# A ring of eight raw weight halves and three rounded ones in a mixture-of-experts layer

## The reference

```python
def hier_moe(h, w_coarse, b_coarse, w_fine, b_fine, w_gate, w_up, w_down):
    t = h.reshape(b * n, d)
    ...
    gates = jnp.sum(jax.nn.one_hot(eidx, N_EXPERTS, dtype=jnp.float32) * pe[..., None], axis=1)
    a = (jax.nn.silu(jnp.einsum('td,edf->tef', t, w_gate))
         * jnp.einsum('td,edf->tef', t, w_up) * gates[:, :, None])
    y = jnp.einsum('tef,efd->td', a, w_down)
```

## Time and profile before

| | us |
|---|---|
| median of 3 runs | 905.15 |
| lowest, highest | 894.86, 905.91 |
| the profiled execution, its own time | 903.03 |
| its span | 900.8 |
| TensorE busy in the span | 863.3 (96%) |
| VectorE busy | 680.5 (76%) |
| ScalarE busy | 461.2 (51%) |
| DMA share in the expert loop | 0.95 to 1.00 |

### The profile page before, as it was taken

The page is one execution under the profiler, slowest core; times in us unless marked ns, Lnnn a source line. Parts: engine busy times, 40 slices in busy tenths (PEclk is TensorE's granted clock), DMA queues, the critical chain, the costliest instruction groups (busy, mean ns, idle before and its releaser), DMA issues.

```text
span 900.8 us, 12158 instructions
## 1 busy us (share of the span) xinstructions
PE 863.3 (96%) x4477; PEld 685.4 (76%) x4477; DVE 680.5 (76%) x1018; ACT 461.2 (51%) x693; POOL 229.7 (25%) x210
## 2 busy tenths in 40 slices
PE   4999999999998999999999999999999999999996
PEld 3789999999996555578888667777777767777653
DVE  5557876968856777466888758988888888888678
ACT  6541211111125777534453618786777677776533
POOL 1000000000024777623021231323322332222141
PEclk9899999999999999999999979999999999999999
DMA  9731526424200112152121589999999999998296
GB/s 369 311 120 44 216 67 241 169 89 164 68 29 29 49 48 102 9 210 94 47 94 48 238 290 334 381 381 380 371 379 366 374 371 361 360 366 333 104 377 255
DMA packets 42003, 194.55 MB, mean 216 GB/s; under 512 B 12150, under 2 KB 13110, under 8 KB 25046
## 3 DMA queue, kind: packets, MB, share of 16 engines
q1 hardware_dynamic: 32232, 174.24, 51.5%
q0 software_dynamic: 9712, 19.52, 5.8%
HBM read 182.00 MB, written 26.41 MB: 231 GB/s over the span
## 4 chain that ended last, share of the span: by engine, by line
PE 75%; DMA 7%; DVE 7%; ACT 4%; issue 3%; POOL 2%; POOLq 0%; SPq 0%; DVEq 0%; ACTq 0%
PE PS L968 9%; PE PS L970 8%; PE PS L972 8%; DMA w_gu<-in_w_gu 5%; PE PS L2474 5%; PE PS L2475 5%; PE PS L2476 5%; PE PS L2508 4%; PE PS L1774 3%; PE PS L1776 3%; PE PS L1775 3%; PE PS L1112 3%; PE PS L1081 3%; PE PS L1132 3%; PE PS L2463 2%
## 5 line engine op out<-in xcount | busy, mean ns | idle before, releaser
L2279 DVE TENSOR_TENSOR gu_lo<-w_gu,gu_hi 128x2048 fp32r<-128x2048 f32 x62 | 141.8, 2287 | 28.4 <-ACT gu_hi L2165 28.4
L968 PE MATMUL PS<-h_hi,w_hi 128*128 128x384 f32 (+1 forms) x432 | 148.3, 343 | 2.5 <-DVE h_lo L677 1.9
L2165 ACT ACTIVATE gu_hi<-w_gu 128x2048 fp32r<-128x2048 f32 x62 | 118.9, 1917 | 58.0 <-DMA w_gu<-in_w_gu 57.9
L970 PE MATMUL PS<-h_lo,w_hi 128*128 128x384 f32 (+1 forms) x432 | 147.0, 340 | 0.0
L972 PE MATMUL PS<-h_hi,w_lo 128*128 128x384 f32 (+1 forms) x432 | 146.5, 339 | 0.0
L2474 PE MATMUL PS<-gu_hi,xT_hi 128*128 128x512 f32 x256 | 103.3, 403 | 1.2 <-DVE xT_lo L2338 1.2
L2475 PE MATMUL PS<-gu_lo,xT_hi 128*128 128x512 f32 x256 | 100.4, 392 | 0.0
L2476 PE MATMUL PS<-gu_hi,xT_lo 128*128 128x512 f32 x256 | 100.2, 391 | 0.0
L2109 POOL DMA_INDIRECT y_rows<-yrows,tab x31 | 37.3, 1202 | 211.4 <-DVE yrows L2311 211.4
L968 PEld LDWEIGHTS PS<-h_hi,w_hi 128*128 128x128 f32 x432 | 81.8, 189 | 8.8 <-issue 7.6
L970 PEld LDWEIGHTS PS<-h_lo,w_hi 128*128 128x128 f32 x432 | 82.3, 191 | 0.0
(11 more groups left out here) (290 smaller groups left out, 1746.7 us busy)
## 6 DMA issues: line engine op xcount, KB each, us to landing
w_gu<-in_w_gu SPq DMA_DIRECT2D x64, 1024.0 KB, 13.8
w_d<-in_w_down SPq DMA_DIRECT2D x32, 1024.0 KB, 13.3
wm<-in_w_mod SPq DMA_DIRECT2D x16, 1024.0 KB, 5.3
w_raw<-in_w_in SPq DMA_DIRECT2D x18, 512.0 KB, 6.3
yt<-y_rows SPq DMA_DIRECT2D x9, 1024.0 KB, 15.2
xt<-in_x_all SPq DMA_DIRECT2D x9, 512.0 KB, 3.6
y_all<-yt SPq DMA_DIRECT2D x9, 512.0 KB, 3.0
wm<-in_w_mod SPq DMA_DIRECT2D x2, 2048.0 KB, 12.5
```

What stands on the lines that cost most here:

```text
L968: pe.matmul(o, w_hi[b][:, k, :], h_hi[:, k, tok], start=k == 0, stop=False)
L970: pe.matmul(o, w_hi[b][:, k, :], h_lo[:, k, tok], start=False, stop=False)
L2165: act.activation(gu_hi[n % 2][:, h, :], w_gu[:, n % 3, h, :], ACT.Copy).then_inc(s_hi, 1)
L2279: dve.tensor_tensor(gu_lo[:, n % 3, h, :], w_gu[:, n % 3, h, :], raw(gu_hi[n % 2][:, h, :]), ALU.subtract).then_inc(s_lo, 1)
```

## The change

The raw halves become a ring of eight (six in the places of `w_gu`, two new ones, `gu_raw6` and `gu_raw7`; the low parts likewise), and the rounded halves a ring of three. `gu_hi1` has one half instead of two, `g2row` one row instead of two, and `fg` and the second row of g2 are loaded after the loop into `xrows`. ScalarE rounds the first half of expert n+2 after silu(n), and the second half after the blend; VectorE makes the low part of the first half after product(n). Two counts of the filler matmuls change, and the order of the tiles in the tail.

```diff
                 pe.wait_ge(s_comb, NT + 1)
-                keep_busy(4, 3)
+                keep_busy(6, 3)
                 pe.wait_ge(s_both, 4)
...
-                keep_busy(4, 3)
+                keep_busy(3, 3)
...
-        ORDER = [4, 5, 0, 1, 8, 6, 2, 3, 7]
+        ORDER = [0, 1, 2, 3, 8, 4, 5, 6, 7]
+        RING, HIGHS = 8, 3
+        s_half = [*(s for pair in s_wgu for s in pair), s_xt[0], s_xt[1]]
+        half_base = [0] * 6 + [16 * (NT - NT // 2), 16 * (NT // 2)]
...
+            def high_half(i):
+                return gu_hi1[:] if i % HIGHS == 2 else gu_hi0[:, i % HIGHS, :]
...
+                    sp.wait_ge(s_gx[0], 16)
+                    for i in range(6, RING):
+                        load_half(i)
                     sp.wait_ge(s_gx[1], 16)
-                    sp.dma_start(g2row[:].rearrange("p c n -> p (c n)"),
-                                 mod_g2.to_broadcast([P, 2 * D])).then_inc(s_g2row, 16)
-                    sp.dma_start(fg[:], a["final_g"].to_broadcast([P, D])).then_inc(s_p7, 16)
+                    sp.dma_start(g2row[:], mod_g2[:, 0:D].to_broadcast([P, D])
+                                 ).then_inc(s_g2row, 16)
                     for n in range(NE):
-                        if n + 3 < NE:
-                            for h in range(2):
-                                sp.wait_ge(s_gu, 2 * n + h + 1)
-                                load_gu(n + 3, h)
+                        for i in (2 * n, 2 * n + 1):
+                            if i + RING < 2 * NE:
+                                sp.wait_ge(s_gu, i + 1)
+                                load_half(i + RING)
...
+                    sp.wait_ge(s_turnx, NE)
+                    sp.dma_start(fg, a["final_g"].to_broadcast([P, D])).then_inc(s_p7, 16)
+                    sp.dma_start(g2_ctx, mod_g2[:, D:2 * D].to_broadcast([P, D])
+                                 ).then_inc(s_p7, 16)
...
                     def high(n, h):
-                        act.wait_ge(s_wgu[n % 3][h], 16 * (n // 3 + 1))
-                        if n >= 2:
-                            act.wait_ge(s_gu, 2 * (n - 2) + h + 1)
...
+                        i = 2 * n + h
+                        loaded_half(act, i)
+                        if i >= HIGHS:
+                            act.wait_ge(s_gu, i - HIGHS + 1)
+                        act.activation(high_half(i), raw_half(i), ACT.Copy).then_inc(s_hi, 1)
...
-                        if n + 2 < NE:
-                            high(n + 2, 0)
                         if n == HELD:
                             blend(n - 1)
                         if n:
                             silu(n)
                         if n + 2 < NE:
+                            high(n + 2, 0)
                             xhigh(n + 2)
-                            high(n + 2, 1)
                         if 1 <= n < HELD:
                             blend(n - 1)
+                        if n + 2 < NE:
+                            high(n + 2, 1)
...
                             turned_low(n - 1)
-                        if n + 2 < NE:
-                            low(n + 2, 0)
                         if n == HELD:
                             out(n - 1)
                         if n:
                             product(n)
+                        if n + 2 < NE:
+                            low(n + 2, 0)
                         if n + 2 < NE:
                             xlow(n + 2)
```

More of the change, by code:

```diff
@@ L1968, in build @@
         HELD = NE - 1
-        ORDER = [4, 5, 0, 1, 8, 6, 2, 3, 7]
+        ORDER = [0, 1, 2, 3, 8, 4, 5, 6, 7]
+        RING, HIGHS = 8, 3
+        GU_LAP = len(range(0, 2 * NE, RING))
+        s_half = [*(s for pair in s_wgu for s in pair), s_xt[0], s_xt[1]]
+        half_base = [0] * 6 + [16 * (NT - NT // 2), 16 * (NT // 2)]
         DVE_SUM = ORDER[1]
@@ L1977, in build @@
             sb6 = allocator(st, "right")
-            g2row = sb6("g2row", [P, 2, D])
-            fg = sb6("fg", [P, D])
+            g2row = sb6("g2row", [P, D])
+            with ExitStack() as same:
+                gu_raw6 = allocator(same, "right")("gu_raw6", [P, HALF])
+            gu_lo6 = sb6("gu_lo6", [P, HALF], F32R)
+            fg, g2_ctx = xrows[:, 1, :], xrows[:, 2, :]
             with ExitStack() as same:
@@ L1983, in build @@
             sb6("gu_hi0_again", [P, 2, HALF], F32R)
-            gu_hi = [gu_hi0, sb6("gu_hi1", [P, 2, HALF], F32R)]
+            gu_hi1 = sb6("gu_hi1", [P, HALF], F32R)
+            with ExitStack() as same:
+                gu_raw7 = allocator(same, "right")("gu_raw7", [P, HALF])
+            gu_lo7 = sb6("gu_lo7", [P, HALF], F32R)
             xT_hi = sb6("xT_hi", [P, 2, KD, P], F32R)
@@ L1997, in build, with raw_half, low_half, loaded_half @@
             held_id = sb6("held_id", [P, 1])
-            held_hi, held_lo = gu_hi[1][:, 0, 0:D], gu_hi[1][:, 1, 0:D]
+            held_hi, held_lo = gu_hi1[:, 0:D], gu_hi1[:, D:2 * D]
+            def raw_half(i):
+                s = i % RING
+                return w_gu[:, s // 2, s % 2, :] if s < 6 else [gu_raw6, gu_raw7][s - 6][:]
+            def low_half(i):
+                s = i % RING
+                return gu_lo[:, s // 2, s % 2, :] if s < 6 else [gu_lo6, gu_lo7][s - 6][:]
+            def high_half(i):
+                return gu_hi1[:] if i % HIGHS == 2 else gu_hi0[:, i % HIGHS, :]
+            def loaded_half(eng, i):
+                eng.wait_ge(s_half[i % RING], half_base[i % RING] + 16 * (i // RING + 1))
             def held_rows(t):
@@ L2033, in _, with load_half @@
                     sp.wait_ge(s_tab, 4)
-                    def load_gu(n, h):
-                        sp.dma_start(w_gu[:, n % 3, h, :], a["w_gu"][n, h]
-                                     ).then_inc(s_wgu[n % 3][h], 16)
+                    def load_half(i):
+                        sp.dma_start(raw_half(i), a["w_gu"][i // 2, i % 2]
+                                     ).then_inc(s_half[i % RING], 16)
                     def load_d(n):
                         sp.dma_start(w_d[:, n % 3, :], a["w_down"][n]).then_inc(s_wd[n % 3], 16)
+                    sp.wait_ge(s_gx[0], 16)
+                    for i in range(6, RING):
+                        load_half(i)
                     sp.wait_ge(s_gx[1], 16)
-                    sp.dma_start(g2row[:].rearrange("p c n -> p (c n)"),
-                                 mod_g2.to_broadcast([P, 2 * D])).then_inc(s_g2row, 16)
-                    sp.dma_start(fg[:], a["final_g"].to_broadcast([P, D])).then_inc(s_p7, 16)
+                    sp.dma_start(g2row[:], mod_g2[:, 0:D].to_broadcast([P, D])
+                                 ).then_inc(s_g2row, 16)
                     for n in range(NE):
-                        if n + 3 < NE:
-                            for h in range(2):
-                                sp.wait_ge(s_gu, 2 * n + h + 1)
-                                load_gu(n + 3, h)
+                        for i in (2 * n, 2 * n + 1):
+                            if i + RING < 2 * NE:
+                                sp.wait_ge(s_gu, i + 1)
+                                load_half(i + RING)
                         if 1 <= n and n + 2 < NE:
@@ L2073, in _ @@
                         if t < 6:
-                            sp.wait_ge(s_gu, 2 * (NE - [2, 1, 3][t // 2] + 1))
+                            sp.wait_ge(s_gu, max(i for i in range(2 * NE) if i % RING == t) + 1)
                         else:
@@ L2201, in blend @@
                             act.wait_ge(s_zero, 16)
-                        act.activation(yrows[:, n % 2, :], g2row[:, 0, :], ACT.Identity,
+                        act.activation(yrows[:, n % 2, :], g2row[:], ACT.Identity,
                                        bias=of_ctx[:, n:n + 1], scale=no_ctx[:, n:n + 1]
@@ L2240, in one_expert @@
                         def one_expert(e, m):
-                            act.wait_ge(s_wgu[0][0], 16 * LAP + 16 * m + 16)
-                            act.activation(gu_hi[0][:], w_gu[:, 0, :, :], ACT.Copy
+                            act.wait_ge(s_wgu[0][0], 16 * GU_LAP + 16 * m + 16)
+                            act.activation(gu_hi0[:], w_gu[:, 0, :, :], ACT.Copy
                                            ).then_inc(s_hi, 1)
@@ L2278, in low @@
                         dve.wait_ge(s_hi, 2 * n + h + 1)
-                        dve.tensor_tensor(gu_lo[:, n % 3, h, :], w_gu[:, n % 3, h, :],
-                                          raw(gu_hi[n % 2][:, h, :]), ALU.subtract
+                        i = 2 * n + h
+                        dve.tensor_tensor(low_half(i), raw_half(i), raw(high_half(i)), ALU.subtract
                                           ).then_inc(s_lo, 1)
@@ L2395, in one_expert @@
                             dve.tensor_tensor(gu_lo[:, 0, :, :], w_gu[:, 0, :, :],
-                                              raw(gu_hi[0][:]), ALU.subtract
+                                              raw(gu_hi0[:]), ALU.subtract
```

(12 more changed lines are left out.)

2 lines of the change are left out of this document (removed).

## The result

The changed kernel takes 934.58 us (median of 4, 933.86 to 935.62); beside it the kernel before took 903.05 (median of 4). The ratio on record is 1.038, with a 95% interval of 1.033 to 1.043: 3.8% slower (the two medians divided give 1.035). I had forecast 931 and 2.9% slower. The time lies in my range, the ratio on record lies above it: 937 over the 905.15 that I started from is 1.035.

A forecast was written before the change was run, and what follows sets the result against it. The prediction took TensorE to bound the expert loop, with late weights costing about 5 us. From 903.03 us, + 37.1 (rounded halves) - 5.0 (ring) - 4.5 (fillers) = 930.6, kept as 931; range 908 to 937.

The forecast's parts named there:

- The direction and the mechanism: Expert loop: slower, as three rounded halves make a rounding wait and delay turned_low, stalling TensorE; + 37.1 us.
- G: Mark in the expert loop: the end on TensorE of the first half of gate and up of an expert.
- The opposite rival (the chain hides): Expert loop: the operations queued behind the wait cost TensorE nothing and the larger ring pays; 893.5 us, chance 0.14.
- The period: Time per expert in the loop: claimed to grow from 9.75 to 11.03 us, by 1.28 us.
- The rest of the walk: Loop, from ScalarE's start at G + 0.20 through down_high, down_low, low and turned_low to TensorE going on at G + 6.78.
- "- 4.5" for the fillers: Routing: two more calls of dummy matmuls close TensorE's idle gap and keep its clock up; 4.5 us saved, 0.9 without.
- The start value: Time of the kernel before that the forecast was divided by: 905.15 us, the median of three.
- The prologue, at nothing: Before the loop: two extra halves loaded ahead of the row of g2; priced at 0, up to 3 us if uncovered.
- The ring, - 5: Expert loop: eight raw halves instead of six end the waits for late weights; 5 us saved, bounds 0 and 5.6.
- The loop and the end: Expert loop and tail: + 37.1 us for the rounded halves, - 5.0 for the ring of raw halves, the end at nothing.

The follow-up runs named there:

- e1: Changed kernel with the second half's rounding moved behind turned(n) on ScalarE: 896.06 us, ratio 0.995 to the kernel before.
- e2: Changed kernel with turned_low(n) moved ahead of low(n+2, 1) on VectorE, ScalarE left as it is: 897.07 us, ratio 0.998 to the kernel before.
- e6: Kernel before with the new orders of ScalarE and VectorE, each rounding waiting for one finished half more, buffers unchanged: 937.19 us, ratio 1.042.
- e9: Kernel before with only the new counts of filler matmuls (6 and 3): 900.10 us against 900.03 before, ratio 0.998.
- e4: Changed kernel with the old counts of filler matmuls (4 and 4): 936.07 us, ratio 1.041 to the kernel before.
- e7: Changed kernel with turned_low first on VectorE, as in e2, and six raw halves instead of eight: 894.42 us, ratio 0.996 to the kernel before.
- e11: Same as e10 but with six raw halves instead of eight: 892.94 us, ratio 0.992 to the kernel before.
- e10: Changed kernel with both moves (those of e1 and e2) and the row of g2 loaded first, eight raw halves: 891.90 us, ratio 0.991 to the kernel before.
- e8: Same kernel as e10, measured in an earlier group: 891.34 us, ratio 0.991 to the kernel before.
- e5: Kernel before with only the new orders of ScalarE and VectorE, buffers and waits unchanged: 897.2 us, ratio 0.996.

## Why the prediction was right and where it was off

**The direction and the mechanism were right.** That three places make high(n+2, 1) wait for G, and that down_high, down_low, low and turned_low stand behind it, is shown by e1, e2 and, from the other side, by e6. The opposite rival (the chain hides) is what e1 and e2 measure, at 896 and 897 against its 893.5; what had to be changed for it was the place of one operation.

**The period was a little short.** I had 11.03 us; it is 11.09. ScalarE starts 0.26 after G, not 0.20, which I had taken from SP's queue. The rest of the walk from there to TensorE's restart (6.58 us, as walked) and the six products (1.49 for 1.50) came as forecast.

**The step that failed is the sum's "- 4.5" for the fillers.** It was read from one execution with a fall of the clock, and taken from a time that stands for executions with and without one. Against those at 0.993 or more, where the changed kernel's four lie too (0.995 to 0.997), the term is nothing: 898.0 + 2.4 + 29.2 + 4.8 = 934.4, where the changed kernel has 934.6. e9 puts the term at nothing that can be told from noise, e4 at 1.5. In the profiled pair the first expert does start 4.7 us earlier, the size that I forecast, but that is partly luck: 2.4 of it come from the clock at 25 to 50 us, which the fillers do not touch, and only 2.3 from the stretch after it.

**The start value stood high.** I divided by 905.15, the median of three; the kernel before has a median of 900.5 in the 72 executions beside the experiments. So 931 over 905.15 made 2.9%, and 934.6 over 900.5 makes 3.8%: some 4 us of the miss are the changed kernel's and some 4 to 5 the start value's. I had read the 894.86 among the three times as spread; by its time it belongs to the executions at the higher clock.

**"The prologue, at nothing"** was the second term off: + 2.4 in the ramp. I had let the row of g2 land within 5.5 us; it took 8.5 (535.49 to 543.98), and the low part of the second half of expert 1 stands behind VectorE's wait for it.

**"The ring, - 5"** came to the right number for the wrong reason. The late halves vanish in the changed kernel since its slow loop leaves the loads time (e6, with six raw halves and the same slow loop, has no wait for weights either), and they would cost nothing in a fast loop either, once the order is mended (e7, e11). The ring as such bought nothing that these runs can tell.

The loop and the end came to + 34.0 us (29.2 + 4.8) where I had + 32.1. With + 2.4 and no 4.5, this makes the 4.1% above the executions of the kernel before at 0.993 or more, and 3.8% above all of them.

**A version that beats both.** e10 (and e8) takes 891.9 us, 0.9% under the kernel before; e11 does so with six raw halves, 892.9.

## What to carry to other kernels

When a ring is cut by one, find the use that its oldest entry now waits for, and list everything queued behind that waiter on its own engine and on the engines after it; the price is the length of that chain against the time the bound engine has before it asks. Put the short operation that the bound engine needs ahead of the long one that it does not need yet: it was worth 37 us here, and it made a larger buffer unnecessary. A term read from one execution must be held against the spread of the runs, and against a second trace, to see whether that execution has something that the others lack; and where two traces differ at a mark, look first at whether they differ before the change can act.

## What the runs showed of the hardware

The granted clock's fall at about 510 to 530 us depends on the execution, not only on the instructions: with the same 1.51 us of idle time before the same products it fell to 0.50 in the kernel before and in e4 and stayed at 1.00 in e5. The fall costs 4.6 us here (33.2 less 28.6 from the load to the first product). The Trainium skill, "TensorE: Matmul & The Clock Gate", Part 1, calls the number of slow matmuls at a kernel's start variable from run to run. These traces agree near the start, where the clock of 25 to 50 us is 1.00 in five and 0.86 to 0.93 in nine, and they show the same for a fall in mid-kernel, which seven of fourteen have (three of the four with the old counts, four of the ten with the new).
